# Hybrid decoder block: the gate projection moves from the mixers' steps into the front's pairs, and z's products are spread through the step

## What is computed

```python
u = rms_norm(x, norm_mix_pre_w)
proj = u @ w_in
z, xbc, dt_raw, q, k, v, gate_ssd, gate_attn = _split(proj, IN_SIZES)
xbc = jax.nn.silu(causal_dwconv(xbc, ssd_conv_w, ssd_conv_b))
...
y = ssd_chunked(xh, dt, a, bm, cm)
y = gated_group_rms_norm(y.reshape(b, s, SSD_D_INNER).astype(x.dtype), z, ssd_norm_w)
y_ssd = y @ ssd_w_out
q = apply_rope(...); k = apply_rope(...)
y_attn = sliding_window_sink_attention(q, k, v, attn_sinks) @ attn_w_out
merged = jax.nn.sigmoid(gate_ssd) * y_ssd + jax.nn.sigmoid(gate_attn) * y_attn
x = x + rms_norm(merged @ w_mix_out, norm_mix_post_w)
```

## Time and profile before

| | us |
|---|---|
| median of 3 runs | 2077.04 (2076.82 to 2079.41) |
| profiled execution, its own time | 2077.58 |
| its span | 2075.9 |
| front, from the start to pair 2 | 109.61 |
| pairs 2 to 16, to the last product | 109.61 to 432.19 |
| last product to the mixers' first matmul | 432.19 to 448.61 |
| mixers, first to 32nd product of B and C | 448.61 to 1019.42 |

### The profile page before, as it was taken

The page is one execution under the profiler, slowest core; times in us unless marked ns, Lnnn a source line. Parts: engine busy times, 40 slices in busy tenths (PEclk is TensorE's granted clock), DMA queues, the critical chain, the costliest instruction groups (busy, mean ns, idle before and its releaser), DMA issues. The chain is left out here.

```text
span 2075.9 us, 27004 instructions
## 1 busy us (share of the span) xinstructions
PE 2012.1 (97%) x9612; PEld 1625.5 (78%) x9612; DVE 1339.8 (65%) x1812; ACT 968.4 (47%) x1815; POOL 603.2 (29%) x445
## 2 busy tenths in 40 slices
PE   6999999989999999999999999999999999999997
PEld 6777877867777777777678888888888888888886
DVE  6878787766666666666634445569877787753523
ACT  5633543535665565655633223335444444444432
POOL 6533234244444354444300000024222222100000
PEclk9999999999999999999999999999999999999999
DMA  4334244364443444433454333222212221455443
GB/s 157 91 112 142 92 134 151 100 203 139 129 139 120 139 143 129 139 109 113 151 200 167 124 145 142 105 80 82 91 66 86 91 89 62 165 175 184 121 147 91
DMA packets 168396, 262.00 MB, mean 126 GB/s; under 512 B 18656, under 2 KB 109152, under 8 KB 168288
## 3 DMA queue, kind: packets, MB, share of 16 engines
q1 hardware_dynamic: 129568, 208.15, 31.5%
q0 software_dynamic: 8368, 30.94, 4.4%
q10 hardware_dynamic: 30352, 21.50, 3.2%
HBM read 191.73 MB, written 63.57 MB: 123 GB/s over the span
## 5 line engine op out<-in xcount | busy, mean ns | idle before, releaser
L2792 DVE TENSOR_TENSOR lt_d_lo<-lt_w_raw,lt_d_hi 128x640 fp32r<-128x640 f32 (+1 forms) x62 | 55.3, 892 | 133.4 <-ACT lt_d_hi L2491 133.3
L1538 POOL TENSOR_TENSOR mx_seg<-mx_seg,mx_cbm 128x1024 f32<-128x1024 f32 x31 | 75.2, 2426 | 168.4 <-ACT mx_seg L1635 168.4
L162 PE MATMUL ps_zg<-u_hi,g_hi 128*128 128x512 f32 x256 | 109.8, 429 | 1.9 <-DVE g_lo L1212 1.9
L162 PE MATMUL ps_zg<-z_w,u_hi 128*128 128x512 f32 x256 | 103.9, 406 | 3.6 <-DVE z_w L1714 3.6
L2362 POOL TENSOR_TENSOR lt_t_f<-lt_w_raw 128x512 f32<-128x512 f32 x21 | 29.1, 1387 | 261.7 <-DVE lt_t_lo L2720 260.2
L2491 ACT ACTIVATE lt_d_hi<-lt_w_raw 128x640 fp32r<-128x640 f32 (+1 forms) x62 | 49.1, 792 | 118.6 <-PE lt_ps L164 102.9
L164 PE MATMUL ps_zg<-u_hi,g_lo 128*128 128x512 f32 x256 | 102.2, 399 | 0.0
L163 PE MATMUL ps_zg<-u_lo,g_hi 128*128 128x512 f32 x256 | 101.8, 398 | 0.0
L164 PE MATMUL ps_zg<-z_w,u_lo 128*128 128x512 f32 x256 | 100.3, 392 | 0.0
L163 PE MATMUL ps_zg<-z_w,u_hi 128*128 128x512 f32 x256 | 99.8, 390 | 0.0
L2449 ACT ACTIVATE lt_t_hi<-lt_t_f 128x512 fp32r<-128x512 f32 x84 | 52.4, 628 | 100.1 <-PE lt_ps L164 61.9
(11 more groups left out here) (553 smaller groups left out, 6612.1 us busy)
## 6 DMA issues: line engine op xcount, KB each, us to landing
lt_w_raw<-in_w_up SPq DMA_DIRECT2D x44, 512.0 KB, 4.5
work<-acs_s SPq DMA_DIRECT2D x32, 512.0 KB, 4.2
lt_sig<-gate_s SPq DMA_DIRECT2D x24, 512.0 KB, 3.5
lt_w_raw<-in_w_down SPq DMA_DIRECT2D x32, 384.0 KB, 3.2
ff_s<-lt_fo SPq DMA_DIRECT2D x21, 512.0 KB, 5.4
tok_s<-fr_xt SPq DMA_DIRECT2D x20, 512.0 KB, 3.2
lt_w_raw<-in_w_down SPq DMA_DIRECT2D x32, 320.0 KB, 3.0
g_raw<-in_w_gate SPq DMA_DIRECT2D x16, 512.0 KB, 6.7
```

The lines of the kernel that those rows point to most:

```text
L162: pe.matmul(dst, s_hi, m_hi, start=first, stop=False, skip_group_check=onto)
L1538: pool.tensor_tensor(seg[:], (carry.a_row[:, 0] if opening else seg[:]), cbm[:].unsqueeze(1).to_broadcast([P, HPG, P]), ALU.mult).then_inc ...
L2792: dve.tensor_tensor(down_w(m)[1][:, 0:n], w_raw[:, m % 2, 0:n], down_w(m)[0][:, 0:n].bitcast(F32), ALU.subtract).then_inc(dw_lo_done, 1)
```

## The change

The eight gate pairs ("g", 16 tiles of 128 channels) become entries of `ORDER`, computed as the other pairs are, copied by `taken` and stored by SP. The last pair of the front is now a gate pair and not one of `xbc`. In the mixers `gate`, `gate_tile`, `store_gate` and `split_gate` are gone; both banks of `carry.ps` now hold z, by turns, and its 24 matmuls are issued as pieces 0 / 1 / 2 to 4 / 5 to 7 at four places of the step (`ahead`), at c = 7 as one piece for the next group. The front ends with z of step 0 and the first four pieces of z of step 1 where it had a first part of a gate tile. Table work of the front sits at other pairs (2, 4, 6, 8 became 3, 6, 9, 12). `w_attn_out` is loaded where the gate's last weights were.

```diff
         self.z_in = [sem(f"z_in{i}") for i in range(2)]
-        self.g_in = [sem(f"g_in{i}") for i in range(2)]
+        self.out_in = [sem(f"out_in{i}") for i in range(2)]
...
-ORDER = (("c", 0), ("c", 1), ("r", 0), ("c", 8), ("r", 4), ("c", 10), ("c", 2), ("c", 3), ("r", 1), ("c", 4), ("c", 9),
-         ("r", 2), ("c", 5), ("c", 6), ("c", 7), ("r", 3), ("c", 11))
+ORDER = (("c", 0), ("c", 1), ("g", 0), ("r", 0), ("c", 8), ("g", 1), ("r", 4), ("c", 10), ("g", 2), ("c", 2), ("c", 3),
+         ("r", 1), ("g", 3), ("c", 4), ("c", 9), ("r", 2), ("g", 4), ("c", 5), ("c", 6), ("g", 5), ("c", 7), ("g", 6),
+         ("c", 11), ("r", 3), ("g", 7))
 N_PAIRS = len(ORDER)
...
         kind, v = ORDER[n // 2]
-        self.n, self.j, self.conv, self.i = n, n % 2, kind == "c", n // 2
-        self.f = 2 * v + self.j
+        self.n, self.j, self.i, self.f = n, n % 2, n // 2, 2 * v + n % 2
+        self.conv, self.rot, self.gate = (kind == k for k in "crg")
...
-        slots = (ps_x[:, 0], carry.ps[:].rearrange("p a n -> p (a n)"), ps_x[:, 1])
+        slots = (ps_x[:, 0], ps_x[:, 1], carry.ps[:].rearrange("p a n -> p (a n)"))
...
+            if before.gate:
+                eng.wait_ge(g_stored[before.j], 16 * (before.gate_n + 1))
...
+                if kind == "g":
+                    return A["w_gate"][2 * v + b]
...
+            def store_gate(n):
+                t = tiles[n]
+                sp.wait_ge(kept, t.kept_n + 1)
+                sem = carry.g_late if t.i == LAST else g_stored[t.j]
+                sp.dma_start(gate_s[t.f], xc[:, t.j]).then_inc(sem, 16)
...
+                    if t.gate:
+                        store_gate(t.n)
...
-            sp.wait_ge(product_done, OPS * (LAST - 1))
-            for j in range(2):
-                sp.dma_start(carry.g_raw[:, j], A["w_gate"][j]).then_inc(carry.g_in[j], 16)
...
-            store_features(2 * LAST)
-            store_features(2 * LAST + 1)
+            store_gate(2 * LAST)
+            store_gate(2 * LAST + 1)
...
-            act.wait_ge(carry.g_in[0], 16)
-            act.wait_ge(product_done, OPS * (i - 1) + 5)
-            act.activation(carry.g_hi[:, 0], carry.g_raw[:, 0], ACT.Copy).then_inc(carry.g_hi_done, 1)
             taken(2 * i + 1)
-            silu(2 * i)
-            silu(2 * i + 1)
...
-            finish(2 * i, range(1, 2))
             c12(i)
-            finish(2 * i, range(2, TAPS))
-            dve.wait_ge(carry.g_hi_done, 1)
-            dve.tensor_tensor(carry.g_lo[:, 0], carry.g_raw[:, 0], carry.g_hi[:, 0].bitcast(F32),
-                              ALU.subtract).then_inc(carry.g_lo_done, 1)
-            finish(2 * i + 1)
...
-            pe.wait_ge(rot_kept, totals["r"])
+            pe.wait_ge(kept, tiles[2 * LAST - 1].kept_n + 1)
...
-            pe.wait_ge(carry.g_lo_done, 1)
-            for k in range(4):
-                matmul3(pe, carry.ps[:, 1], carry.g_hi[:, 0, k], carry.g_lo[:, 0, k], u_hi[:, k, 0:HALF],
-                        u_lo[:, k, 0:HALF], k == 0, False)
...
+            for k in range(AHEAD):
+                matmul3(pe, carry.ps[:, 1], u_hi[:, k, P:2 * P], u_lo[:, k, P:2 * P], carry.z_hi[:, k], carry.z_lo[:, k],
+                        k == 0, False)
...
-        ps_z, ps_g = carry.ps[:, 0], carry.ps[:, 1]
+        ps_z = carry.ps
...
-            def gate_tile(g, c, first, ending=False):
-                j, n = c % 2, NT * g + c
-                act.wait_ge(gate_done, n + 1)
-                if not (first and c < 2):
-                    act.wait_ge(g_stored[j], 16 * (4 * g + c // 2))
-                act.activation(g_out[:, j], ps_g[:], ACT.Copy).then_inc(gate_out, 1)
-                if not ending:
-                    store_gate(g, c)
...
-            def split_gate(w, use):
-                act.wait_ge(g_in[w], 16 * (use + 1))
-                act.activation(g_hi[:, w], g_raw[:, w], ACT.Copy).then_inc(g_hi_done, 1)
...
-            def gate(g, c, ks, opening):
-                j, w = c % 2, (c // 2) % 2
-                if ks[0] == 0:
-                    pe.wait_ge(g_lo_done, 4 * g + c // 2 + 1)
-                    if not opening:
-                        pe.wait_ge(gate_out, NT * g + c)
-                    if g == 0 and c == 1:
...
+            def z(g, c, ks):
+                n = NT * g + c
+                if ks[0] == 0 and n >= 2:
+                    pe.wait_ge(z_used, n - 1)
+                if g == 0 and c == TH and ks[0] == 0:
+                    pe.wait_ge(carry.u_back, 32)
...
-                    last = matmul3(pe, ps_z[:], u_hi[:, k, c * P:(c + 1) * P], u_lo[:, k, c * P:(c + 1) * P],
+                    last = matmul3(pe, ps_z[:, c % 2], u_hi[:, k, c * P:(c + 1) * P], u_lo[:, k, c * P:(c + 1) * P],
...
+                    def ahead(*ks):
+                        if c < NT - 1:
+                            z(g, c + 1, range(*ks))
+
                     if not opening:
-                        gate(g, c, range(0, 4), opening)
+                        ahead(0, 1)
...
-                    gate(g, c, range(4, 6), opening)
                     if not opening:
+                        ahead(1, 2)
                         pe.wait_ge(p_ready, n)
...
-                    gate(g, c, range(6, KT), opening)
+                    ahead(AHEAD if opening else 2, 5)
...
-                    next_z(g, c, last_group, range(KT))
+                    ahead(5, KT)
+                    if c == NT - 1 and not last_group:
+                        z(g + 1, 0, range(KT))
```

More of the change, by code:

```diff
@@ L31 @@
 TH = NT // 2
+AHEAD = 4
 KH = KT // 2
@@ L272, in __init__, with front @@
         counts["k", self.j] += self.turns
-        counts["q", self.j] += not self.conv
+        counts["q", self.j] += self.rot
+        counts["g", self.j] += self.gate
 def feature_tiles():
-    counts = {"c": 0, "r": 0, "t": 0, **{(what, j): 0 for what in "fkq" for j in range(2)}}
+    counts = {**{k: 0 for k in "crtn"}, **{(k, j): 0 for k in "fkqg" for j in range(2)}}
     return [Tile(n, counts) for n in range(2 * N_PAIRS)], counts
-def front(nc, A, v_s, q_s, u_s, acs_s, feat_s, tok_s, ident, utri, band, ones, consts_done, u_hi, u_lo,
+def front(nc, A, v_s, q_s, u_s, gate_s, acs_s, feat_s, tok_s, ident, utri, band, ones, consts_done, u_hi, u_lo,
           dt_v, acs, ea, decay, cdecay, carry):
@@ L399, in slot_free @@
             else:
-                eng.wait_ge(rot_kept, before.rot_n + 1)
+                eng.wait_ge(kept, before.kept_n + 1)
         def xc_free(eng, n):
@@ L407, in xc_free @@
             before = tiles[n - 2]
-            if not before.conv:
+            if before.rot:
                 eng.wait_ge(q_stored[before.j], 16 * (before.q_n + 1))
+            if before.gate:
+                eng.wait_ge(g_stored[before.j], 16 * (before.gate_n + 1))
             if before.turns:
@@ L419, in xt_free @@
                 return
-            before = next((t for t in reversed(tiles[:n]) if t.j == n % 2 and (t.turns or not t.conv)), None)
+            before = next((t for t in reversed(tiles[:n]) if t.j == n % 2 and (t.turns or t.rot)), None)
             if before.conv:
@@ L517, in _ @@
                 a, b = tiles[2 * i - 2], tiles[2 * i - 1]
-                if not a.conv:
+                if a.rot:
                     swap(b.n)
@@ L664, in _ @@
             for i in range(1, LAST):
-                if not tiles[2 * i - 2].conv:
+                if tiles[2 * i - 2].rot:
                     by_sine(2 * i - 2)
@@ L1042, in c12, with finish @@
                     dve.tensor_tensor(bank(1, 1), bank(1, 1), u2[:], ALU.add).then_inc(tile_ready, 1)
-            def finish(n, taps=range(1, TAPS)):
+            def finish(n):
                 t = tiles[n]
                 dve.wait_ge(tap_done, t.conv_n + 1)
-                for k in taps:
+                for k in range(1, TAPS):
                     if k > 1:
@@ L1181, in _ @@
                 c22(i)
-                if not a.conv:
+                if b.rot:
                     lo_t3(i + 1)
                     rotate(b.n)
-                if i == 6:
+                if i == 9:
                     table_by_heads()
@@ L1457, in group @@
                 for c in range(NT):
-                    if c % 2 == 0:
-                        u = 4 * g + c // 2
-                        if not (last and c == NT - 2):
-                            src = A["w_attn_out"][0] if last and c == NT - 4 else A["w_gate"][u + 2]
-                            sp.wait_ge(g_lo_done, u + 1)
-                            sp.dma_start(g_raw[:, (c // 2) % 2], src).then_inc(g_in[(c // 2) % 2], 16)
+                    if last and c == NT - 4:
+                        for j in range(2):
+                            sp.dma_start(g_raw[:, j], A["w_attn_out"][j]).then_inc(out_in[j], 16)
                     if last and c == NT - 1:
@@ L1625, in group @@
                         act.wait_ge(sq_done, n)
-                    act.activation(silu[:], ps_z[:], ACT.Exp, scale=-1.0).then_inc(z_exp_done, 1)
```

(15 more changed lines are left out.)

111 lines of the change are left out of this document (43 added, 68 removed).

## The result

The changed kernel takes 2122.72 us (median of 4 runs, 2120.87 to 2124.2) against 2076.93 (4 runs, 2074.86 to 2079.41) of the kernel before on the same chip: ratio 1.022, 95% interval 1.0202 to 1.0237. Slower, by 46 us; the forecast was 2116, slower by 39. The profiled executions differ by 2119.2 - 2075.9 = 43.3 us of span.

A forecast was written before the change was run, and what follows sets the result against it. PE was taken to bound front and mixers before the change, the chain through ACT and DVE the mixers' steps after it. The terms summed to +39.1 us, giving 2116 us; 8 in 10 between 2098 and 2145.

The forecast's parts named there:

- eight pairs, less relief: Front: eight more pairs at 19.04 us, +152.3, less 5 for fewer waits of PE for taps and silu.
- passage: From the front's last product to the mixers' first matmul: last xbc pair's taps and silus go; -6 us, bounds 0 and -8.
- step 0: First mixer step: 36 large matmuls become 12, so a chain decides; -4 us, bounds 0 and -5.
- steps 1 to 30: Mixers: each step falls from 18.39 to 15.15 us, set by the chain through ACT and DVE; -97.2 us.
- step 31 and the rest: End of the mixers: step 31 is on the chain already, only its gate tile's copy goes; -1 us.
- the bounds for the waits: Front: relief of PE's waits for taps and silu lies between 0 and -10.2 us; -5 was taken.
- Rival B: Mixers: the loop through ACT and DVE sets the step at 15.15 us, total 2116 us; chance 0.65.
- A: Mixers: PE stays the bound, the step falls to 13.05 us, total 2053 us; chance 0.08.
- They cancel nearly, as they do now: Change of group in the mixers: c = 7 about 3 us more, c = 0 about 2.5 us less.
- rival D: Mixers: idle stretches make PE's clock fall again and again to 1.2 GHz, +66 us, total 2182; chance 0.06.
- Rival C: Mixers: contention of POOL with DVE, or late loads, costs 0.8 us a step, +24, total 2140; chance 0.14.
- What would make me wrong: Mixers' chain: a link that need not wait for the one before; a third of a us a step is 10 us.

The follow-up runs named there:

- x6: The changed kernel with gate pairs 0 to 6 together behind the last xbc pair and table work at earlier pairs; 2129.00 us, ratio 1.0246.
- x1: The changed kernel with 12 of z's 24 large matmuls a step left out, so its output is not the layer's; 2125.42 us.
- x3: The changed kernel with the scores' mask and max ahead of `opened` on DVE; 2105.53 us, ratio 1.0135 to the kernel before.
- x4: x3 with DVE's min of the next decays also moved ahead of the norm's root; 2088.23 us, ratio 1.0045 to the kernel before.
- x7: x4 with z in pieces 0-1 / 2 / 3-4 / 5-7; 2088.15 us, ratio 1.0056 to the kernel before.
- x2: The changed kernel with z's 24 matmuls in one piece behind the eight into `ps_d`; 2269.39 us.

## Why the prediction was right, point by point

| term | forecast | measured |
|---|---|---|
| eight pairs, less relief | +147.3 | 464.58 - 322.58 = +142.0 |
| passage | -6 | 11.22 - 16.42 = -5.2 |
| step 0 | -4 | 12.22 - 15.37 = -3.2 |
| steps 1 to 30 | -97.2 | 459.31 - 551.75 = -92.4 |
| step 31 and the rest | -1 | +2.1 |
| sum | +39.1 | +43.3 |

*The front.* The gate pair costs 19.04 us, as forecast. The pairs took 10.3 us less than 152.3 more, where the forecast had 5. Of this 8.0 are fewer waits: PE is idle for 5.6 us in all pairs and was for 13.6 (322.58 - 308.99), of which taps and silu had 10.2. The other 2.3 are less busy time than eight pairs cost by 19.04, at a granted clock of 1.00 against 0.99. I took the middle of the bounds for the waits; the far end was nearer. x6 shows that most of it hangs on where the gates and the table work stand. The pair's price stands in rows of pair 12; those that carry the turns of an xbc pair before them take longer.

*The chain.* Rival B was the forecast and is what happened, link by link, at 15.15 against a measured 15.17 (x1 excludes A; x3 and x4 shorten the step by moving links of the chain alone). The prediction's idle time of PE, 2.1 us a step, stands in the brackets as 0.42 + 0.35 + 0.84 = 1.6. By the distance between starts, which is what a wait costs on PE, it is 0.50 + 0.53 + 1.00 = 2.0: `ps_f` starts 0.82 us behind the last matmul of z where the earlier trace rows's kernel had 0.32, `ps_e` 0.76 and the turn 1.23 where 0.23 is usual.

*The term that was mis-sized* is that of steps 1 to 30, by 4.8 us of 97.2. "They cancel nearly, as they do now" held for the two steps that it speaks of: the three steps c = 7 took 20.0, 18.5 and 17.6, 10.7 us more than three of 15.15, and the three c = 0 behind them 11.8 each, 10.1 us less. What the sum left out stands beside them. The steps c = 1 took 15.9 to 16.3, 2.6 us in all, where they had been 0.45 us shorter than a middle step each, and step 30, where the splits for the last output weights stand ahead of mask and `y_t`, took 16.7, 1.6 us more.

In all three steps c = 1 `yn`, a link of the chain, takes 1.50 instead of 0.75 us, and in no other step of the changed kernel. The first of them, with POOL at work on its own instruction (L1527, 722.96 to 724.00):

```profile
723.05 1.50 DVE L1787 SCALAR_TENSOR_TENSOR raw_pieces<-mx_y,mx_stat,mx_norm_row 128x512 f32<-128x512 f32 x1
```

At the steps c = 7 PE decides beside the chain. At the first of them there is no z to issue before `ps_e`, PE waits 2.88 us for `y_t`, and behind it the clock is lower (one z matmul 0.63 us instead of 0.39, and 0.43 us from start to start instead of 0.23):

```profile
695.59 1.10 PE L1887 MATMUL mx_ps_e<-mx_state,work 128*128 128x512 f32 x2 [2.88 <-ACT mx_y_t L1579]
...
700.49 0.63 PE L164 MATMUL ps_zg<-z_w,u_hi 128*128 128x512 f32 x1
```

ACT ends the scalings at 702.74, but the turn starts at 707.19, since all 24 matmuls of the next group's z stand ahead of it. At the other two the turn follows the scalings by 0.5 us. The lower clock is rival D's, in the few steps where a wait is not covered by z; the order on PE comes on top of it.

*The end* was forecast at -1 and reads +2.1, but hardly any of this lies in the mixers. From turn to turn step 31 takes 15.38 us where it took 15.53, although PE waits 3.83 us for `y_t` in it and the window behind the last product of B and C has a granted clock of 0.91. From its turn to the late stage's first product it is 9.16 us against 9.20. The rest, +2.3, lies in the late stage, which the change does not touch and which took between 1034.7 and 1038.2 us in the profiles of all fourteen kernels (the +2.3 is within that scatter). Of the 4.2 us between the sums of forecast and profile more than half is this.

The front came out 5.3 us cheaper than forecast and steps 1 to 30 4.8 us dearer. That these two cancel is luck, and makes the total look closer than its terms.

*Rival C* didn't come in the middle steps: none of them is above 15.23 us. It came in the three steps c = 1, at 0.75 us each as above, and after the min was moved it came in more steps (1.52 for 0.68 us in x7).

*What would make me wrong* was put as a link that need not wait for the one before. There were two such links, in the sense that the order on DVE and not the data made them wait: `opened` ahead of the mask, `yn` ahead of the min. The change left that order alone, so it didn't matter for the forecast; it is worth some 35 us to whoever changes it.

## What to carry to other kernels

Before taking work off a busy engine, read one iteration on the other engines from end to end: the wait of the engine that seems to idle (3.53 us of ACT here) is about all that the move can gain (the step fell by 3.32), and the step's new length is the sum of the links around the loop. Where such a loop becomes the bound, look first for links that only the program order of one engine ties, and expect the next bound to stand close behind (here PE at 13.1, the loads, and the splits at the change of group). A large product that can be cut into pieces is worth most as cover in the waits of a stage of short matmuls: in x2 the lack of this cover cost as much by the clock (78 us) as by the idle time (67).
